# Moving the softmax scaling from ScalarE to GpSimd in a two-layer hybrid encoder step (float32, one core)

## The reference, cut to what matters

```python
logits = jnp.einsum('bqngd,bqknd->bqngk', qg, k_sel) * (HEAD_DIM ** -0.5)
logits = jnp.where(valid[:, :, None, None, :], logits, -jnp.inf)
p = jax.nn.softmax(logits, axis=-1)
o = jnp.einsum('bqngk,bqknd->bqngd', p, v_sel)
```

## Time and profile before

| what | value |
|---|---|
| median of 3 runs | 1529.4 us |
| the profiled execution, its own time | 1529.4 us |
| its span (first to last instruction) | 1527.6 us |
| TensorE busy, mean granted clock | 1245.7 us, 0.861 |
| VectorE busy | 752.2 us |
| ScalarE busy | 377.2 us |
| GpSimd busy | 384.5 us |
| attention stage of layer 0, of layer 1 | about 335 to 446 us, 1086 to 1191 us |

### The profile page before, as it was taken

One profiled execution on the slowest core, in us unless ns is written; L12 is line 12 of the kernel. 1 busy time (PEld: TensorE's weight loads), 2 busy tenths in 40 slices (PEclk: granted clock), 3 DMA queues, 4 the chain that ended last, 5 costly groups with the idle time before them and its releaser, 6 DMA issues. The chain is left out here.

```text
span 1527.6 us, 13612 instructions
## 1 busy us (share of the span) xinstructions
PE 1245.7 (82%) x4971; PEld 730.9 (48%) x4971; DVE 752.2 (49%) x1541; ACT 377.2 (25%) x836; POOL 384.5 (25%) x212
## 2 busy tenths in 40 slices
PE   3699888946999879999807997896668996999980
PEld 0354525432445466777505544362335454777760
DVE  1109999787615531111152199998684353311114
ACT  2111231235551111111131003312547211211112
POOL 0005999430000020000020079995000011000002
PEclk7799999965799969999958998598557997999995
DMA  9971385240770369999681003011003016699975
GB/s 359 321 255 56 117 285 191 108 177 1 241 277 28 138 227 375 367 364 364 208 302 29 9 28 118 0 63 55 9 1 76 0 55 227 207 364 367 368 260 189
DMA packets 139297, 274.41 MB, mean 180 GB/s; under 512 B 16308, under 2 KB 98588, under 8 KB 132830
## 3 DMA queue, kind: packets, MB, share of 16 engines
q1 hardware_dynamic: 110272, 199.31, 37.8%
q10 hardware_dynamic: 22398, 50.63, 9.8%
q0 software_dynamic: 6560, 23.60, 4.3%
HBM read 237.89 MB, written 52.40 MB: 190 GB/s over the span
## 5 line engine op out<-in xcount | busy, mean ns | idle before, releaser
L409 PE MATMUL ps<-W,arena 128*128 128x256 f32 (+1 forms) x1280 | 346.7, 427 | 7.9 <-ACT arena L1100 2.8
L409 PEld LDWEIGHTS ps<-W,arena 128*128 128x128 f32 x1280 | 241.6, 193 | 82.7 <-issue 53.3
L419 PE MATMUL ps<-C,arena 128*128 128x128 f32 (+3 forms) x851 | 135.4, 311 | 112.0 <-DVE arena L1322 25.8
L409 PE MATMUL ps<-W,hT 128*128 128x512 f32 (+5 forms) x640 | 192.7, 462 | 1.4 <-DVE gt L1175 1.4
L419 PEld LDWEIGHTS ps<-C,arena 128*128 128x128 f32 (+3 forms) x851 | 113.0, 167 | 151.2 <-issue 58.5
L1249 DVE SCALAR_TENSOR_TENSOR arena<-arena,taps 128x606 f32<-128x606 f32 x180 | 158.9, 951 | 0.2
L409 PEld LDWEIGHTS ps<-W,hT 128*128 128x128 f32 (+1 forms) x640 | 103.0, 182 | 91.5 <-issue 82.4
L409 PE MATMUL ps<-hT,W 128*128 128x64 f32 (+1 forms) x512 | 140.7, 438 | 3.4 <-ACT hT L868 3.4
L1619 POOL TENSOR_TENSOR arena<-arena 128x512 f32<-128x512 f32 x8 | 89.6, 11195 | 210.8 <-ACT arena L897 210.8
L647 PE MATMUL ps<-W,hT 128*128 128x512 f32 (+1 forms) x320 | 141.4, 595 | 1.0 <-issue 1.0
L1646 POOL DMA_INDIRECT x_d<-arena,sid x30 | 28.6, 954 | 444.7 <-DVE sid L1462 421.1
(11 more groups left out here) (217 smaller groups left out, 1150.7 us busy)
## 6 DMA issues: line engine op xcount, KB each, us to landing
W<-in_w_ada SPq DMA_DIRECT2D x48, 1024.0 KB, 5.9
W<-in_w_gate SPq DMA_DIRECT2D x32, 1024.0 KB, 10.6
W<-in_w_up SPq DMA_DIRECT2D x32, 1024.0 KB, 13.0
W<-in_w_down SPq DMA_DIRECT2D x32, 1024.0 KB, 7.8
arena<-x_d SPq DMA_DIRECT2D x33, 512.0 KB, 10.9
y_d<-arena ACTq DMA_DIRECT2D x33, 512.0 KB, 7.3
W<-in_w_in SPq DMA_DIRECT2D x16, 1024.0 KB, 14.7
W<-in_w_out SPq DMA_DIRECT2D x8, 1024.0 KB, 6.9
```

What stands on the lines that cost most here:

```text
L409: ins = T.matmul(out, l, r, start=n == 0, stop=n == len(pairs) - 1, skip_group_check=True)
L419: count(T.transpose(o, i, ident[0:m, 0:m]), done if n == len(outs_ins) - 1 else None)
```

## The change

The multiplication by the inverse sums leaves ScalarE and becomes four GpSimd TENSOR_SCALAR instructions for each group, in place on the same rows. GpSimd runs all ten groups in order behind its normalisation of the queries and ahead of the scatter. ScalarE's exponentials of group n+2 get one more wait, for the inverses of group n-2, since they overwrite the sums that those inverses read.

```diff
-                def normalised(n):
-
-                    t, g = GROUPS[n]
-                    m = rows_of(t)
-                    act.wait_ge(L["inv"], n + 1)
-                    for i in range(4):
-                        h = S_INV + 4 * (n % 2) + i
-                        r = PR[0:m, 4 * (n % 2) + i, 0:NKEYS[t]]
-                        ins = S.mul(r, r, small[0:m, h:h + 1])
-                    ins.then_inc(L["pn"], 1)
-
...
                 exps(0)
                 exps(1)
-                normalised(0)
...
-                    if n + 1 < len(GROUPS):
-                        normalised(n + 1)
                     if n + 2 < len(GROUPS):
+                        if n >= 2:
+                            act.wait_ge(L["inv"], n - 1)
                         exps(n + 2)
...
                 rope(pool, G, qkr, *PARTS[0], 19760, L["pch"], n_chain, L["ropeq"], 1)
 
+                for n, (t, g) in enumerate(GROUPS):
+                    m = rows_of(t)
+                    pool.wait_ge(L["inv"], n + 1)
+                    for i in range(4):
+                        h = S_INV + 4 * (n % 2) + i
+                        r = PR[0:m, 4 * (n % 2) + i, 0:NKEYS[t]]
+                        ins = G.tensor_scalar(r, r, small[0:m, h:h + 1], None, ALU.mult)
+                    ins.then_inc(L["pn"], 1)
```

## The result

The change made the kernel slower. In runs on one chip the kernel before took 1530.62 us (1529.12 to 1538.32, 8 runs) and the changed one 1539.62 us (1535.74 to 1542.50, 8 runs): ratio 1.0054, 95% interval 1.0035 to 1.0074. The forecast was 1535.0 against 1529.4, +5.6 us; measured are +9.0 us by the medians, and the interval allows 5.4 to 11.3.

The account below looks back on a forecast made before the run. No single engine bounds attention: VectorE's search paces rounds 0 to 3, later TensorE and ScalarE alternate (layer 0: TensorE alone). Layer 1's 4.2 plus layer 0's 1.9 us on 1529.4 gave 1535.5, rounded to 1535; range 1526.5 to 1541.

Parts of the forecast that it names:

- ScalarE's relief is worth nothing: Attention, both layers: removing 40 multiplications per layer from ScalarE gains nothing, as the exponentials' wait for VectorE hides it.
- The price of a burst from L1634: GpSimd's four multiplications per group: 2.98 ns an element, so 6.9 us at 576 keys, 1.5 at 128.
- Rival 1: GpSimd runs the short form, 0.84 us for 606 elements, and no waits meet: 1525.2 us; chance 0.12.
- Group 0 gains 1.0 us: First group's transposes: a GpSimd burst of 1.5 us lets TensorE start 1.0 us earlier.
- Group 2's transposes late but hidden behind the copies: Layer 1: first transpose piece 0.9 us late, hidden since the second piece waited 2.92 us for ScalarE's copies.
- VectorE's small operation waits for GpSimd: Before the exponentials, VectorE's four-element operation waits up to one GpSimd instruction; layer 1's shift reaches +3.7 us by group 8.
- Group 9 late by another 0.5 us: End of layer 1's attention: the burst ends at 1192.1, TensorE wanted 1191.6, so the shift goes from +3.7 to +4.2.
- a smaller risk at the upper end: Where TensorE idles more, its granted clock may fall to 1.2 GHz (0.5); counted only in the range's upper end.
- Layer 0 +1.9, its tail hidden: Layer 0's attention: +1.6 up to group 4, then about +0.3; from 412 us on TensorE has no gaps to lose.
- A late stage ends everything late by as much: After each attention stage: output projection and experts follow, so the delay carries through in full; together 6.1 us.
- Rival 3: GpSimd's instructions are stretched, bursts of 8.9 and 7.9 us at 576 and 512 keys: 1541 us; chance 0.10.
- Rival 2: VectorE's small operations don't wait for GpSimd, only the inverse, multiplication, transpose chain counts: 1527.8 us; chance 0.28.

Follow-up runs that it names:

- both: Changed kernel with a second multiplication, by ones, in each GpSimd instruction and the negation as a tensor_reduce; 1530.03 us, ratio 1.0002 to the kernel before.
- zero: Multiplication by the inverse sums left out altogether, TensorE's transposes waiting for the inverse alone; 1527.02 us, ratio 0.9984 to the kernel before.
- twoop: Changed kernel with a second multiplication, by ones, in each GpSimd instruction; 1531.04 us, ratio 1.0000 to the kernel before.
- nolock: Changed kernel with VectorE's four-element negation ahead of the exponentials written as a tensor_reduce; 1536.15 us, ratio 1.0040 to the kernel before.
- dummy: Kernel before, plus the same forty multiplications per layer on GpSimd on words nobody reads, nothing on the chain waiting; 1533.66 us, ratio 1.0023.
- split: Changed kernel with group 9, the last, multiplied on ScalarE again; 1533.31 us, ratio 1.0030 to the kernel before.
- fill_before: Kernel before with eight unread TensorE products on constants in each of rounds 2 to 9 of layer 1; 1530.51 us, ratio 1.0011.
- fill_after: Changed kernel with eight unread TensorE products in each of rounds 2 to 9 of layer 1; 1535.86 us, ratio 1.0042 to the kernel before.
- warm_both: Changed kernel with unread products in TensorE's long early gaps, both layers, two-operation GpSimd form and negation as tensor_reduce; 1525.28 us, ratio 0.9978 to the kernel before.
- warm_before: Kernel before with unread products in TensorE's long gaps around the first attention rounds of both layers; 1513.95 us, ratio 0.9892.

## Why the prediction was right, point by point

- **ScalarE's relief is worth nothing: right, shown.** ScalarE has 20 us less in each stage, and both, with short bursts and no locking, is at 1.0002, within 2.8 us to each side. Zero puts the ceiling of the whole step at 2.5 us.
- **The price of a burst from L1634, the single-operation form: right for the long ones, too low for the short.** 1716 and 1563 ns against 1.71 and 1.52 us, but 922 ns against 0.76 at 256 keys and 610 against 0.38 at 128. Rival 1 had the price of the other form right (0.81 us at 576 elements) and twoop ran it; its time, 4.2 us faster, was wrong: 0.0%. I had doubted it for a good reason, since the added instruction has one operation.
- **Group 0 gains 1.0 us: wrong, 0.05 us in each layer.** A 128-element multiplication takes 0.61 us, not 0.38, so the burst is 2.4 us and not 1.5; I had scaled one row at 606 elements down by a factor of 4.7 through zero. ScalarE had begun 1.35 us after the inverse and taken 1.26 us, 2.6 us together; GpSimd's 2.4 us and the way to it come to the same. In the sum this gain met the maximum's wait of 1.0 us for tile 4, which didn't happen either: two errors that cancel.
- **Group 2's transposes late but hidden behind the copies: right**, 0.97 us of wait and a second piece with no shift. Group 7 waits 0.47 us for GpSimd and group 4 0.22, which I hadn't listed; the waits for copies behind them take these up.
- **VectorE's small operation waits for GpSimd: right in kind, too large.** For layer 1, I had four meetings of the negation, 1.6, 0.3, 0.9 and 0.9 us, 3.7 in all; there were three, of 0.52, 0.24 and 0.12, 0.9 in all. Each wait that I took ended with a GpSimd instruction; of the six measured in both layers two did, and four ended in the middle of one. The first, forecast at 1.6 us, came where I said, in the fourth instruction of the burst, and ended 0.76 us after that instruction's start instead of with it. Nolock and dummy give an estimate of 2 to 3.5 us for the mechanism in both layers. The sentence that I cited from the Trainium skill (SBUF — State Buffer, "Who interferes with whom") names the right pair of engines. Its exclusion for a whole instruction is what those two waits look like and not what the other four do: they ended 0.71 to 0.76 us into instructions of 1.56 and 1.72 us.
- **Group 9 late by another 0.5 us: too small.** The wait rose by 1.16 us, of which 0.5 is the price of the burst (3.6 us and not 3.1), and transposes and values behind it ran at 1.2 GHz, 0.9 us each, and the start of the output projection 2.1 us longer. In split's profile none of this is left. I had named the clock as a smaller risk at the upper end; it belonged in this term, since two waits, now of 1.74 and 1.59 us, stand right before these rows.
- **Layer 0 +1.9, its tail hidden: not settled.** The stage was 4.0 us longer. Its three lengthened negations make 1.3 us, but where TensorE slips it is the clock. Rows of TensorE in layer 0, before and then after:

```profile
391.69 3.26 PE L575 MATMUL ps<-arena 64*128 64x512 f32 x7
394.88 1.92 PE L439 MATMUL ps<-W,scT 128*32 128x512 f32 x16
```
```profile
392.98 5.73 PE L575 MATMUL ps<-arena 64*128 64x512 f32 x7
398.64 3.64 PE L439 MATMUL ps<-W,scT 128*32 128x512 f32 x16
```

  The stage had slipped by only 0.2 us when the first of these rows began (1.29 less the 1.1 at its start), and then the same instructions took 4.2 us longer. But fill_before, whose layer 0 is unchanged, shows the long form at that place too, and its stage is 1.8 us shorter than that of before:

```profile
392.00 5.81 PE L575 MATMUL ps<-arena 64*128 64x512 f32 x7
397.74 3.64 PE L439 MATMUL ps<-W,scT 128*32 128x512 f32 x16
```

  Low here, its clock was high in the next round. So where in the stage the clock falls shifts between executions of the same code, and one profile can't say what of the 4.0 us is the change's. The other kernels with long bursts (nolock, dummy, split, fill_after) have 113.1 to 113.5 us in this stage, before, zero and fill_before 111.0, 110.5 and 109.2, twoop and both 108.3 and 108.4: some 2 to 5 us for the long burst. That the forecast's 1.9 is at the edge of this is luck: all of it was locking, and nolock has 113.2 us without one lengthened negation.
- **A late stage ends everything late by as much: right between the layers, not behind the second.** The stretch between the stages is 639.7 us before and 639.9 after. That they agree to 0.2 is chance: with the same code there zero's profile has 637.5 us and twoop's 642.3. Behind the second stage 2.6 us more were lost, 2.1 of them in the projection's first instructions.
- **The rivals.** Rival 3's stretched bursts didn't come (6.8 and 6.2 us at 576 and 512 keys, not 8.9 and 7.9), though its 1541 us lies closest to the measured time. Rival 2 was wrong on the negation, and its 1527.8 us too. The measured 1539.62 us lies 1.1 us above the forecast's own range (1531.5 to 1538.5); the kernel before was 1.2 us slower in these runs too.

The sum came out low by 3.4 us with errors of both signs in it. In layer 1, +4.2 was forecast and +4.9 measured, but 3.7 of the forecast was locking and 0.9 of the measured; group 9 with its clock gave 2.9 (1.16, 0.88 and 0.89) instead of 0.5. Most of the missing 1.1 us is the clock once more, in the values of group 4 and the transposes of group 5, before and then after:

```profile
1161.14 2.99 PE L613 MATMUL ps<-arena,vrow 128*64 128x256 f32 x16
1164.06 1.09 PE L419 MATMUL ps<-C,arena 128*128 128x128 f32 x8
```
```profile
1167.12 3.68 PE L613 MATMUL ps<-arena,vrow 128*64 128x256 f32 x16
1170.73 1.52 PE L419 MATMUL ps<-C,arena 128*128 128x128 f32 x8
```

So the sign and the engine that causes the loss were forecast rightly, and that the size came near is in good part luck: locking, priced at 5.6 us in both layers where the negations lost 2.2, stood in for the clock, which the sum left out. The term that failed most is locking, the one left too small is group 9. What the runs show is that the length of the GpSimd instruction is the cause (twoop takes all of the loss away). That it works through two ways, the locking (dummy: 1 to 6 us) and the chain with the clock behind it (split, about 3.7 us), is shown by dummy for the first and fits the rows for the second, for which split's interval is too wide. How the 9.0 us divide between them stays open, for the intervals of these runs are 2 to 3 us wide to each side. Open too: why the one-operation form takes twice as long, why some of the negation's waits end in the middle of a GpSimd instruction, and why warm_both doesn't reach warm_before.

## What to carry to other kernels

Price a moved step with the exact form that the new engine will run, at two sizes, since a single row scaled to a smaller tile leaves out the fixed part; and try the neighbouring forms, for here a second, idle operation halved the time at 512 and 576 elements. A step between two waits is latency, not load: an idle engine that does it more slowly costs time even when the busy one is relieved. What follows the wait can cost more than the wait: look at the clock of the rows behind it, past the end of the stage too. Where TensorE's granted clock is low in a stage with gaps, products that nobody reads, put into the gaps, can pay for themselves: here they gave 1.1% where the move lost 0.5. Where they stand matters: spread over rounds 2 to 9 of one layer they gave nothing (ratio 1.0011).

## What the runs showed of the hardware that I had not expected

- GpSimd's TENSOR_SCALAR in float32 with one operation and a column of scalars takes 1716 ns for 64x576, 1563 for 128x512 and 610 for 128x128; with two operations 813, 767 and 444.
- A 128x4 TENSOR_SCALAR on VectorE beside such a GpSimd instruction can take 0.29 to 0.71 us instead of 0.17. In the changed kernel two of six such waits ended with the GpSimd instruction (within 0.03 us), and four 0.71 to 0.76 us after its start. As TENSOR_REDUCE the operation never took over 0.158 us, and a two-input maximum of 64x4 in the middle of a burst took its usual 0.15.
- Some 15 us of added matmuls in the gaps of a 105 us stage moved the kernel by 0.11%, with an interval that includes zero, and the granted clock of that stage from 0.64 to 0.75.
